# A padding of 32 bytes ahead of the arena in a two-block transformer kernel

## Chip, cores and metric

One core of a Trainium2 chip runs the kernel. The metric is device time in microseconds for one execution, lower is better.

## The reference

Two transformer blocks run on one sequence of 512 tokens with 1024 channels, in float32. The first block has two layers. Each modulates x by conditions, projects it (`h @ w_in`), and mixes three branches: attention over 512 latent and 256 context tokens, a depthwise convolution of 31 taps with a layer norm, and a pooling over windows of 2 to 16 tokens. Then comes a gated feed-forward part. Layer 0 treats the 256 context tokens as well, 768 tokens in all; layer 1 treats 512.

```python
def conv_ffn(h, w_up, dw_w, dw_b, w_down):
    a, u = jnp.split(h @ w_up, 2, axis=-1)
    a = depthwise_conv(a, dw_w, dw_b)
    return (jax.nn.silu(a) * u) @ w_down
```

The second block also has two layers: latent attention and gated linear attention side by side, an output product, and a gate of the residual: `h + sigmoid(rmsnorm(h) @ w_ple_gate) * (p @ w_ple_proj)`.

## The kernel before, in words

Activations lie with channels in the 128 partitions and tokens along the row: eight chunks of 128 channels, each `TOK` = 768 floats long. Every large product is done in three fp32r products, high part by high part, high by low and low by high. So an activation stands as a pair (`act_hi`, `act_lo`), and so does a weight (`w_hi`, `w_lo`). Weights come in units of 128 x 1024 floats (one output chunk): the SP queue loads a unit into `w_raw`, ACT rounds it to `w_hi` (line 1244), POOL or DVE subtracts to get `w_lo` (lines 479, 1931, 1937), and TensorE uses it. A ring of four units is in flight.

On TensorE a unit is eight chunks by three products. `unit` (line 595) issues them product by product; `first_pair` (line 530) interleaves the first two units of a stage that has to wait for its activations chunk by chunk; `first_four` (line 544) does it with four units and `unit_by_chunk` (line 644) with one. In layer 0 each chunk takes a matmul of 512 columns and one of 256 with the same weights; in layer 1 and in the second block one of 512.

```python
def unit(s, tile, sp_, kt, hi, lo, within=None):
    for n, (w, act) in enumerate(((WH, hi), (WL, hi), (WH, lo))):
        ...
        for k in range(kt):
            for a, b in sp_:
                last = nc.tensor.matmul(tile(a, b), w[:, s * UNIT + k * P:s * UNIT + (k + 1) * P],
                                        act[:, k * TOK + a:k * TOK + b],
```

The stages of a layer of the first block are, in order: conv, gate0, qkv, attn (and attn_ctx in layer 0), u, mix, gate2, gate1, pw, out, then up0, down0, up1, down1, up2, down2. The pool mixing (mix) multiplies fp32 operands of the arena (line 857). The feed-forward part has 22 chunks of 128, cut into parts of 8, 8 and 6. A stage up_p makes a part's chunks (16, 16 and 12 units), DVE convolves them (lines 2378, 2381), ACT applies silu (line 1574), DVE multiplies (line 2389) and splits the product into `ffn_hi` and `ffn_lo` (lines 1903, 1905), and the stage down_p multiplies these by eight units of 8, 8 and 6 chunks (line 877). DVE adds its result to x (line 1990). down_p begins with `first_pair`; its other six units come from `unit`. In down2 the sums of the layer norm stand between the units. The convolution's taps run on DVE beside the products (lines 2142, 2150): an even tap reads the arena at an offset of one float per tap.

In the second block the products are issued at line 902. Its last stage, pg, multiplies `u2_hi` and `u2_lo` by eight units in each of two layers.

Memory: tensors are laid one behind another in a partition, each start rounded up to 32 bytes. x, act_hi, act_lo, w_raw, w_hi, w_lo and tmp come first, and all start at multiples of 64. Some small tensors follow, then the masks, then the arena, 20280 floats, which is the last. It starts at 148192 = 64 x 2315 + 32. The names below are three views of the same memory:

```python
        ARENA_N = 20280
        with nc.sbuf_tensor("arena", [P, ARENA_N], f32) as AR:
            pass
        with nc.sbuf_tensor("ffn_hi", [P, CH * TOK], f32r) as GH, nc.sbuf_tensor("ffn_lo", [P, CH * TOK], f32r) as GL:
            pass
```

`u2_hi` and `u2_lo` follow in the same way. ffn_hi and u2_hi start where the arena starts; ffn_lo and u2_lo follow them by multiples of 64 bytes. Within the arena most operands lie at multiples of 16 floats. Exceptions are the convolution's sum and inputs, and the sums of the layer norms (offset 13832 = 16 x 864 + 8).

The order of the work is fixed by the program: each engine runs its own list, and semaphores hold it until its inputs are there.

Of the kernel before, what the change touches and what calls it, by code (L numbers as in the profile page):

```python
# [131 lines left out]
def two_blocks(nc, weights, ada_w, pool_w, vec1_d, vec2_d, gla_w_d, x_d, cond_d, ple_d, pos_d, consts_d, rope_d,  # L132
# [4 lines left out]
    with ctx:  # L137
        def sb(name, n, dt=f32):
            return ctx.enter_context(nc.sbuf_tensor(name, [P, n], dt))
# [28 lines left out]
        Q_EPS = CST[:, 3:4]  # L168
        MASK = sb("gla_masks", 2 * P, i32)
        ARENA_N = 20280  # L170
        with nc.sbuf_tensor("arena", [P, ARENA_N], f32) as AR:
            pass

# [35 lines left out]
        CLN_R = CONV_IN  # L209
        QR = ARENA_N - HEADS * TOK // P  # L210
        LN_R_BACK = CONV_SUM
# [2674 lines left out]
```

How the kernel before makes its waits and increments, by code:

```python
        @block.sync  # L399
# [7 lines left out]
            def unit_load(r, s):  # L407
                sp.wait_ge(units_split, r * SLOTS + s - 1)
                sp.dma_start(RAW[:, (s % 2) * UNIT:(s % 2 + 1) * UNIT],
                             weights[bass.ds(r * SLOTS + s, 1)].rearrange("o p n -> p (o n)")).then_inc(raw_landed[s % 2], 16)
# [8 lines left out]
            for i in range(ADA_FIRST // 2):
                ada_early_load(i)
            for dst, src in ((VEC1T, vec1_d), (IDENT, consts_d[0]), (PERM, consts_d[1]), (ONES, consts_d[2])):
                sp.dma_start(dst[:, :], src).then_inc(loaded, 16)
            sp.dma_start(RC[:, :], consts_d[3][:, 0:64]).then_inc(loaded, 16)
            for i in range(ADA_FIRST // 2, ADA_FIRST):
                ada_early_load(i)
            for s in range(2):
                sp.dma_start(RAW[:, s * UNIT:(s + 1) * UNIT], weights[s]).then_inc(raw_landed[s], 16)
            sp.wait_ge(on(0, "cond"), 1)
            for k, landed in enumerate((x_half, cond_loaded)):
                part = slice(k * CH // 2 * TOK, (k + 1) * CH // 2 * TOK)
                sp.dma_start(X[:, part], x_d[:, part]).then_inc(landed, 16)
# [16 lines left out]
                        unit_load(r + (RING[l, st] + (s + 3) // SLOTS), (s + 3) % SLOTS)  # L449
                        for a in range(first + s * n, first + (s + 1) * n):
                            sp.wait_ge(on(0, "ada_used"), r * (SLOTS * n // 2) + (a // 2 + ADA_STEPS - 1))
                            if a % ADA_SLOTS == 3:
```

## Time and profile before

| | us |
|---|---|
| median of 3 runs | 3226.6 |
| the runs | 3226.60, 3230.95, 3224.77 |
| span of the profiled execution, from the first to the last instruction | 3229.0 |
| TensorE busy in it | 3124.9 |
| DVE, ACT, POOL busy | 1947.2, 1140.8, 805.5 |

Of the profiled execution only the span is given; no time around it is shown. A matmul's record overlaps the next one's, since matmuls are pipelined, so the pace of a stage is read from starts and not from durations. In the timeline an entry merges neighbouring matmuls of the same operands, and x8 or x16 is a group: one product of a unit, eight chunks of 512 columns or eight pairs of 512 and 256.

### The profile page before, as it was taken

How to read it: one execution, taken by the hardware profiler on the slowest of the kernel's cores; microseconds unless marked ns; L12 is line 12 of the kernel's file. 1: busy time of each engine (PE TensorE's matmuls, PEld its weight loads, DVE VectorE, ACT ScalarE, POOL GpSimd, SP SyncE). 2: the span in 40 equal slices, each digit the busy share in tenths (PEclk: the TensorE clock that was granted, in tenths of full speed). 3: DMA queues.
4: the chain of work that ended last, by engine and by line, in shares of the span. 5: the costliest groups of instructions: out<-in, count | busy, mean ns of one | idle time of the engine just before them, and what ended most of it. 6: DMA issues, size and time to landing. Idle time of an engine off the chain costs nothing.

```text
span 3229.0 us, 43667 instructions
## 1 busy us (share of the span) xinstructions
PE 3124.9 (97%) x16074; PEld 2482.6 (77%) x16074; DVE 1947.2 (60%) x2707; ACT 1140.8 (35%) x1616; POOL 805.5 (25%) x316
## 2 busy tenths in 40 slices
PE   7999999999999999999999999999999999999998
PEld 4778877888878888886777677877886786777775
DVE  4787987654566154356978975663636565255443
ACT  3122254234232221124333535343223536343543
POOL 0001201232323232331012024402444322233312
PEclk9999999999999999999999999999999999999999
DMA  7442101112111211124531022422323221222211
GB/s 282 170 166 79 40 1 41 51 59 98 59 46 65 66 59 65 60 71 140 202 128 46 1 69 81 134 78 91 98 92 114 66 66 53 65 85 72 85 40 66
DMA packets 75308, 270.52 MB, mean 84 GB/s; under 512 B 8592, under 2 KB 9616, under 8 KB 74512
## 3 DMA queue, kind: packets, MB, share of 16 engines
q1 hardware_dynamic: 71376, 256.04, 23.9%
q10 hardware_dynamic: 3776, 12.32, 1.1%
q8 instruction: 108, 1.77, 0.2%
q14 instruction: 48, 0.39, 0.0%
HBM read 263.87 MB, written 4.46 MB: 83 GB/s over the span
## 4 chain that ended last, share of the span: by engine, by line
PE 86%; DVE 7%; ACT 2%; DVEq 2%; issue 1%; DMA 1%; SPq 0%; ACTq 0%
PE ps L595 50%; PE ps L902 11%; PE ps L530 4%; PE ps L544 2%; PE ps L711 2%; PE ps L834 2%; PE ps L1043 1%; PE ps L732 1%; PE ps L699 1%; PE ps L814 1%; PE ps L1122 1%; PE ps L644 1%; PE ps L602 1%; PE ps L1140 1%; PE ps L857 1%
## 5 line engine op out<-in xcount | busy, mean ns | idle before, releaser
L479 POOL TENSOR_TENSOR w_lo<-w_raw,w_hi 128x1024 fp32r<-128x1024 f32 x312 | 805.3, 2584 | 2389.3 <-ACT w_hi L1244 2389.3
L1244 ACT ACTIVATE w_hi<-w_raw 128x1024 fp32r<-128x1024 f32 x380 | 399.7, 1055 | 572.3 <-PE ps L595 304.8
L595 PE MATMUL ps<-act_hi,w_hi 128*128 128x512 f32 x2544 | 538.4, 361 | 2.3 <-DVE w_lo L1931 0.6
L595 PE MATMUL ps<-act_lo,w_hi 128*128 128x512 f32 x2544 | 521.8, 354 | 0.0
L595 PE MATMUL ps<-act_hi,w_lo 128*128 128x512 f32 x2544 | 521.2, 354 | 0.0
L595 PEld LDWEIGHTS ps<-act_hi,w_hi 128*128 128x128 f32 x2544 | 417.1, 188 | 117.3 <-issue 44.1
L595 PEld LDWEIGHTS ps<-act_hi,w_lo 128*128 128x128 f32 x2544 | 417.4, 188 | 70.3
L595 PEld LDWEIGHTS ps<-act_lo,w_hi 128*128 128x128 f32 x2544 | 417.2, 188 | 70.2 <-issue 0.5
L1990 DVE SCALAR_TENSOR_TENSOR x<-ps,mod,x 128x512 f32<-128x512 f32 x96 | 60.3, 659 | 295.3 <-PE ps L595 238.1
L2150 DVE SCALAR_TENSOR_TENSOR x<-arena,vec,x 128x512 f32<-128x512 f32 x336 | 230.5, 713 | 0.2 <-issue 0.2
L2142 DVE SCALAR_TENSOR_TENSOR arena<-arena,vec 128x783 f32<-128x783 f32 (+1 forms) x240 | 227.8, 949 | 0.0
L2381 DVE SCALAR_TENSOR_TENSOR arena<-arena,vec 128x769 f32<-128x769 f32 (+1 forms) x88 | 143.2, 1627 | 15.4 <-issue 15.4
L1310 ACT ACTIVATE arena<-ps,vec 128x768 f32<-128x768 f32 (+3 forms) x64 | 50.8, 794 | 278.6 <-PE ps L595 192.3
L902 PE MATMUL ps<-act_hi,w_hi 128*128 128x512 f32 x432 | 119.2, 408 | 7.3 <-ACT act_hi L1597 6.2
L2378 DVE TENSOR_SCALAR arena<-arena,vec 128x769 f32<-128x769 f32 (+1 forms) x44 | 29.1, 661 | 140.1 <-ACT arena L1569 140.1
L902 PE MATMUL ps<-act_hi,w_lo 128*128 128x512 f32 x432 | 113.1, 394 | 0.0
L902 PE MATMUL ps<-act_lo,w_hi 128*128 128x512 f32 x432 | 112.6, 392 | 0.0
L834 PE MATMUL ps<-arena 128*128 128x256 f32 (+1 forms) x288 | 103.7, 480 | 4.7 <-ACT tmp L1349 4.7
L1569 ACT ACTIVATE arena<-ps 128x512 f32<-128x512 f32 x66 | 32.4, 525 | 211.2 <-PE ps L595 201.0
L902 PEld LDWEIGHTS ps<-act_hi,w_hi 128*128 128x128 f32 x432 | 79.8, 190 | 34.5 <-issue 17.2
L1905 DVE TENSOR_TENSOR ffn_lo<-arena,ffn_hi 128x768 f32 (+1 forms) x44 | 101.3, 2302 | 6.5
L711 PE MATMUL ps<-arena 128*128 128x256 f32 x416 | 103.1, 381 | 1.6 <-ACT arena L1468 1.5
(343 smaller groups left out, 4490.5 us busy)
## 6 DMA issues: line engine op xcount, KB each, us to landing
w_raw<-in_weights SPq DMA_DIRECT2D x380, 512.0 KB, 3.5
arena<-in_ada_w SPq DMA_DIRECT2D x75, 512.0 KB, 4.7
tmp<-in_ada_w SPq DMA_DIRECT2D x21, 512.0 KB, 4.8
x<-in_x SPq DMA_DIRECT2D x2, 1536.0 KB, 20.0
x<-in_x ACTq DMA_DIRECT2D x1, 3072.0 KB, 10.4
arena<-in_pool_w ACTq DMA_DIRECT2D x2, 1024.0 KB, 4.9
x_mid<-x ACTq DMA_DIRECT2D x1, 2048.0 KB, 7.4
x<-x_mid ACTq DMA_DIRECT2D x1, 2048.0 KB, 8.5
```

The source lines that it names most:

```text
L479: nc.gpsimd.tensor_tensor(WL[:, w], raw, WH[:, w].bitcast(f32), ALU.subtract).then_inc(units_split, 1)
L530: last = nc.tensor.matmul(ps(tb + s, a, b), w[:, s * UNIT + k * P:s * UNIT + (k + 1) * P], act[:, k * TOK + a:k * TOK + b], start=(n == 0 ...
L544: last = nc.tensor.matmul(tile(0, s, a, b), w[:, s * UNIT + k * P:s * UNIT + (k + 1) * P], act[:, k * TOK + a:k * TOK + b], start=(n == 0 ...
L595: last = nc.tensor.matmul(tile(a, b), w[:, s * UNIT + k * P:s * UNIT + (k + 1) * P], act[:, k * TOK + a:k * TOK + b], start=(n == 0 and k ...
L711: last = nc.tensor.matmul(ps(3, (m % 2) * 512, (m % 2) * 512 + 2 * P), values(m, k), AR[:, a:a + 2 * P], start=(k == 0), stop=(k == nk - 1))
L834: last = nc.tensor.matmul(ps(it % 2, a, b), AR[:, q:q + P], AR[:, k + a:k + b], start=True, stop=True)
L902: return nc.tensor.matmul(out, w0[:, k0:k0 + P], act[:, k * n:k * n + SEQ], start=start, stop=stop)
L1244: nc.scalar.activation(WH[:, s * UNIT:(s + 1) * UNIT], RAW[:, (s % 2) * UNIT:(s % 2 + 1) * UNIT], ACT.Copy).then_inc(hi_done, 1)
L1905: return V.tensor_tensor(lo, src, hi.bitcast(f32), ALU.subtract)
L2142: t = V.scalar_tensor_tensor(acc, src, w, acc, ALU.mult, ALU.add)
L2150: t = V.scalar_tensor_tensor(acc, src, w, acc, ALU.mult, ALU.add)
L2381: t = V.scalar_tensor_tensor(cv, src, w, cv, ALU.mult, ALU.add)
```

## The change

A tensor of eight floats, 32 bytes in each partition, is laid between the masks and the arena. Nothing reads or writes it.

```diff
         Q_EPS = CST[:, 3:4]
         MASK = sb("gla_masks", 2 * P, i32)
         ARENA_N = 20280
+        sb("gap_before_arena", 8)
         with nc.sbuf_tensor("arena", [P, ARENA_N], f32) as AR:
             pass
```

The arena, ffn_hi and u2_hi then start at 148224 = 64 x 2316, which is also 256 x 579. All other tensors stay where they are.

## Rows read from the trace of the kernel before

**Rows 1.** The page: span; granted clock in 40 slices; chain by engine.

```profile
span 3229.0 us, 43667 instructions
...
PEclk9999999999999999999999999999999999999999
...
PE 86%; DVE 7%; ACT 2%; DVEq 2%; issue 1%; DMA 1%; SPq 0%; ACTq 0%
```

**Rows 2.** TensorE's waits: us in total, times, longest.

```profile
PE ps L732 <- DMA arena<-in_ada_w: 16.3, 3, 9.3
```

**Rows 3.** TensorE's groups by form: xcount | busy us, mean ns | idle.

```profile
L595 PE MATMUL ps<-ffn_hi,w_hi 128*128 128x512 f32 x264 | 82.1, 399 | 1.7 <-DVE x L1990 1.7
...
L902 PE MATMUL ps<-u_hi,w_hi 128*128 128x512 f32 x128 | 35.3, 399 | 2.3 <-ACT arena L1843 1.8 <-DVE arena L2723 0.5
...
L530 PE MATMUL ps<-ffn_hi,w_hi 128*128 128x512 f32 x88 | 30.9, 396 | 2.3 <-DVE arena L2389 2.3
```

**Rows 4.** TensorE's timeline, layer 1, down1 and up2: start us, us.

```profile
2356.85 2.03 PE L595 MATMUL ps<-ffn_hi,w_lo 128*128 128x512 f32 x8
...
2386.72 2.02 PE L595 MATMUL ps<-ffn_lo,w_hi 128*128 128x512 f32 x8
...
2392.24 1.98 PE L595 MATMUL ps<-act_lo,w_hi 128*128 128x512 f32 x8
...
2452.08 1.98 PE L595 MATMUL ps<-act_lo,w_hi 128*128 128x512 f32 x8
```

**Rows 5.** TensorE's timeline, second block, the gate product (pg).

```profile
2825.43 2.03 PE L902 MATMUL ps<-u_hi,w_lo 128*128 128x512 f32 x8
...
2844.10 2.03 PE L902 MATMUL ps<-u_lo,w_hi 128*128 128x512 f32 x8
```

**Rows 6.** TensorE's timeline, layer 0: down0, then up2.

```profile
1071.66 3.04 PE L595 MATMUL ps<-ffn_hi,w_hi 128*128 128x512 f32 x16 [0.36 <-DVE x L1990]
1074.54 2.96 PE L595 MATMUL ps<-ffn_hi,w_lo 128*128 128x512 f32 x16
...
1119.34 2.96 PE L595 MATMUL ps<-ffn_lo,w_hi 128*128 128x512 f32 x16
...
1400.73 2.94 PE L595 MATMUL ps<-act_hi,w_lo 128*128 128x512 f32 x16
...
1420.14 2.94 PE L595 MATMUL ps<-act_lo,w_hi 128*128 128x512 f32 x16
```

**Rows 7.** TensorE's timeline, layer 0: pw, out and up0.

```profile
779.68 3.05 PE L595 MATMUL ps<-act_hi,w_hi 128*128 128x512 f32 x16 [0.25 <-DVE arena L2315]
782.57 3.00 PE L595 MATMUL ps<-act_hi,w_lo 128*128 128x512 f32 x16
...
819.32 3.00 PE L595 MATMUL ps<-act_lo,w_hi 128*128 128x512 f32 x16
...
848.02 2.23 PE L595 MATMUL ps<-act_hi,w_hi 128*128 128x512 f32 x11 [0.27 <-DVE x L1990]
...
953.85 2.98 PE L595 MATMUL ps<-act_hi,w_lo 128*128 128x512 f32 x16
...
996.25 2.98 PE L595 MATMUL ps<-act_hi,w_lo 128*128 128x512 f32 x16
```

**Rows 8.** The chain in order of time: stage mix, layer 0.

```profile
599.79 20.64 PE ps L857 x64
```

**Rows 9.** Two lines of DVE: xcount: duration ns min/median/max.

```profile
L2142 DVE SCALAR_TENSOR_TENSOR arena<-arena,vec x69: 1023/1030/1036, 61.1 to 277.1; 128x783 f32<-128x783 f32 x69
...
L1905 DVE TENSOR_TENSOR ffn_lo<-arena,ffn_hi x44: 691/2655/3016, 953.1 to 2456.1; 128x768 f32 x22, 128x512 f32 x22
L1905 DVE TENSOR_TENSOR act_lo<-arena,act_hi x12: 691/692/694, 2546.4 to 3107.5; 128x512 fp32r<-128x512 f32 x12
```

**Rows 10.** The page, part 6: DMA issues, KB each, us to landing.

```profile
arena<-in_ada_w SPq DMA_DIRECT2D x75, 512.0 KB, 4.7
tmp<-in_ada_w SPq DMA_DIRECT2D x21, 512.0 KB, 4.8
```

## The prediction

> **What bounds the kernel.** I read the chain that ended last, then TensorE's waits, then its groups by form, then its timeline. The chain is TensorE for 86% of 3229.0 us [rows 1], and its waits are small: the largest is 16.3 us for the first loads [rows 2]. Its clock is granted in full, 2.4 GHz, in all 40 slices [rows 1]. So what counts is the spacing of matmuls in a full queue, and little else. The profiled execution's span, 3229.0 us, lies 2.4 us above the median of the runs, 3226.6; the sum below is a difference, set against the median. About 0.2% (6.5 us) is what a measurement can tell from no change; the three runs themselves lie 6.2 us apart.
>
> **What moves.** No instruction is added, dropped or moved. Every address in the arena, and so in ffn_hi, ffn_lo, u2_hi and u2_lo, grows by 32 bytes; all but a few arena operands go from 32 bytes past a multiple of 64 onto one. act_hi, act_lo, w_hi and w_lo lie on multiples of 64 before and after. The trace of before thus holds both cases of the same instruction.
>
> **Step 1: 512-column fp32r matmuls that stand alone (layer 1, second block).** Starts of groups of eight: from ffn_hi and ffn_lo 16 steps take 2386.72 - 2356.85 = 29.87 us, 1.867 each; from act_hi and act_lo 33 steps take 2452.08 - 2392.24 = 59.84 us, 1.813 each [rows 4]. The gate product from u2 gives 18.67 us in 10 steps, again 1.867 [rows 5]. So a misplaced moving operand costs 0.054 us in eight, 6.7 ns (three per cent) a matmul. Counts: ffn sources have (264 + 88) x 3 = 1056 matmuls of 512 columns over two layers, 528 of them in layer 1; u2 sources have 128 x 3 = 384 [rows 3]. That is 66 + 48 = 114 groups by 0.0535 = **6.1 us less**, all in stages where TensorE hardly waits (1.7, 2.3 and 2.3 us in the three groups [rows 3]). ACT, DVE and POOL deliver weights fast enough for 1.813, since the up stage between the down stages runs at it [rows 4].
>
> The Trainium skill ("TensorE: Matmul & The Clock Gate", section "Back-to-back issue gap") gives a warm matmul N / 2.4 + 2.5 ns, 215.7 ns for 512 columns, with no term for an address. By that rule this step would be worth nothing; the trace disagrees, with 226.7 and 233.3 ns for one shape.
>
> **Step 2: the pairs of layer 0 (512, then 256 columns).** Here the change may lose. Eight pairs from ffn take 44.80 / 16 = 2.800 us in down0; from act they take 19.41 / 7 = 2.773 in up2 [rows 6], but 36.75 / 13 = 2.827 in pw and 42.40 / 15 = 2.827 in up0 [rows 7]. Same instructions and placement, two rhythms, and each lasts for a stage or more. What differs is how the stage starts: pw and out (779.68, 848.02) begin after TensorE stood idle for 0.25 and 0.27 us behind the last first-pair matmul, and fall into the slow one [rows 7]. The down stages begin in just that way (1071.66, idle 0.36, behind x) [rows 6]. Once their operand is placed like act, I expect them at 2.827: 66 groups by 0.027 = **1.8 us more**. Stages up1 and up2 follow without a break. They have 16 + 12 units of three groups, 84, now at 2.773 (rows of up2 stand for both) [rows 6]; up0 held the slow rhythm through all of its units and loop turns [rows 7], so I expect it to be handed on: 84 x 0.0535 = **4.5 us more**.
>
> **Step 3: fp32 matmuls on the arena.** They take two cycles a column: 64 in stage mix, 32 pairs of 768 columns, take 20.64 us [rows 8], 0.645 a pair against 2 x 768 / 2.4 = 640 ns. An operand off its place shows no more than those 5 ns. I take nothing; the bound is 2.5 ns for each of roughly 1500 such matmuls (by the groups by form, those that run four at a time taken as one), 3.8 us less, and nothing excludes 0.5 more. The sums (arena offset 13832, the ln means) move the other way, off a multiple of 64; they are a few of these.
>
> **Step 4: DVE, ACT, POOL.** The taps of line 2142 read at 15 offsets 8 bytes apart and take 1023 to 1036 ns [rows 9], so DVE doesn't see placement. I take nothing; even 13 ns on each of some 1000 instructions lies beside matmuls.
>
> **Step 5: DMA.** 512 KB land in 4.7 us in the arena and 4.8 in tmp [rows 10]. TensorE waits for arena loads three times, 16.3 us, at the start [rows 2]. I take nothing, with 0.1 us for each wait, 0.3, either way.
>
> The Trainium skill ("DMA: Bandwidth & Descriptors", "How a descriptor splits into AXI transactions") says that a start off a 256-byte boundary costs extra beats. The arena goes from 224 past such a boundary onto one, so an estimate by that page is 135 beats falling to 128, 5% off its loads, under 1 us of the first loads' wait. No row here has a load onto such a boundary.
>
> **Sum.** -6.1 + 1.8 + 4.5 = +0.2 us: 3226.8.
>
> **Rivals.**
> (a) The down stages of layer 0 fall into the fast rhythm, so up1 and up2 keep it: -6.1 - 66 x 0.027 = -7.9, 3218.7. For it: up1 and up2 run so now, after ffn stages [rows 6]. Against: both act stages that begin after an idle run slow [rows 7]. 18%.
> (b) The slow rhythm takes the down stages alone, and breaks at the loops of up1 and up2, or in down1 where the start is perturbed: -6.1 + 1.8 = -4.3, 3222.3. 18%.
> (c) Slower: DVE against POOL. ffn_lo takes DVE 0.69 us or up to 3.02 for the same line, act_lo never over 0.69 [rows 9]; I read the long ones as DVE held up while POOL splits weights. A shifted rhythm changes which ones meet. The first pair of each down stage (line 530) waits for them, behind line 2389, now 2.3 us in all [rows 3]. One more on that path costs 3.02 - 0.69 = 2.3 us at most; it decides from three, for which there are six down stages: +0.2 + 6.9, 3233.7. Against: so many long ones exist now (the median is 2.66), and they cost 2.3 us. 6%.
> (d) Placement has no bearing, or the padding is swallowed so the arena stays where it is, and the 6.7 ns come from something else that ffn and u2 share: 3226.6. The Trainium skill's rule quoted in step 1 ends here as well. Against: two tensors, three stages, one figure. 6%.
> My own case has the remaining 52%.
>
> **How the numbers follow.** The time is that of my case. Low: (a) at 3218.7 less the first loads' 0.3 and rounding, 3218. High: my case with 0.5 + 0.3 of unknown costs and the spread of the runs (the highest 3230.95), 3230.5; it leaves out (c) and the lower part of (a). My case's own range is 3223 to 3230.5. Faster by over 0.2% means below 3220.1: nearly all of (a), a little of (b) and, by the bound of step 3, of mine: 0.23. Slower means above 3233.1: (c) and 1% for runs: 0.07. The same: 0.70.
>
> **What would show it.** Groups of eight from ffn in layer 1 and from u2 at 1.813 instead of 1.867 show step 1 right; at 1.867 they show (d). Groups of eight pairs in down0, down1 and down2 of layer 0 at 2.827 and in up1 and up2 at 2.827 show step 2 right; 2.773 in all shows (a), a mix shows (b). Line 857's 20.64 us, line 2142's 1030 ns and the 4.7 us of landing should stay. The forecast fails if the rhythm of layer 0 is set by more than the start, or if a stage that now runs at 2.773 from act (u, gate2) changes its rhythm too: some 48 groups, 2.6 us.

## The result, and the profile after

The change makes the kernel slower: 3233.7 us, median of 21 runs (3228.07 to 3237.16), against 3227.2 for the kernel before, also 21 runs in the same rounds (3223.65 to 3232.44). The ratio is 1.0020, 95% interval 1.0014 to 1.0026. The forecast was 3226.8 with a range of 3218.0 to 3230.5, and 0.07 on "slower". The profiled execution took 3234.3 us, 1.8 more than its span; its span is 3.5 us above that of before [rows 1]. In every run here the time is 1.8 us more than the span, so the profiled execution of before took about 3230.8 us, 3.6 above its median, and that of the change 0.6 above its own: the two profiles show about half of the difference of 6.5 us.

The page after: span, granted clock, chain by engine.

```profile
span 3232.5 us, 43667 instructions
...
PEclk9999999999999999999999999999999999999999
...
PE 86%; DVE 7%; ACT 2%; DVEq 2%; issue 1%; DMA 1%; SPq 0%; ACTq 0%
```

Clock, instruction count and the chain's shares are the same, and DVE and ACT are as busy as before (1947.2 and 1140.7 us), so what differs must lie mainly in how TensorE's matmuls are spaced. All lines past the edit are one higher. TensorE's groups by form (xcount | busy us, mean ns | idle), against [rows 3]:

```profile
L596 PE MATMUL ps<-ffn_hi,w_hi 128*128 128x512 f32 x264 | 81.9, 399 | 1.7 <-DVE x L1991 1.7
...
L903 PE MATMUL ps<-u_hi,w_hi 128*128 128x512 f32 x128 | 35.1, 399 | 2.3 <-ACT arena L1844 1.8 <-DVE arena L2724 0.5
```

Each is 0.2 us less; 6.7 ns on the 132 matmuls of the first that stand alone and on the 128 of the second would be 0.9 us. TensorE's timeline after (start us, us), layer 1 down1 and up2, then the gate product of the second block, against [rows 4, 5]:

```profile
2364.28 2.02 PE L596 MATMUL ps<-ffn_lo,w_hi 128*128 128x512 f32 x8
...
2392.16 2.02 PE L596 MATMUL ps<-ffn_lo,w_hi 128*128 128x512 f32 x8
...
2397.69 1.98 PE L596 MATMUL ps<-act_lo,w_hi 128*128 128x512 f32 x8
...
2424.89 1.98 PE L596 MATMUL ps<-act_lo,w_hi 128*128 128x512 f32 x8
...
2830.87 2.03 PE L903 MATMUL ps<-u_hi,w_lo 128*128 128x512 f32 x8
...
2849.53 2.04 PE L903 MATMUL ps<-u_lo,w_hi 128*128 128x512 f32 x8
```

Eight from ffn now take 27.88 / 15 = 1.859 us (1.867 before), eight from act 27.20 / 15 = 1.813, eight from u2 18.66 / 10 = 1.866. The operand stands on a multiple of 64 and has not become as fast as act. The timeline after for layer 0, up0, down0, the start of up1, and up2, against [rows 6, 7]:

```profile
955.10 2.93 PE L596 MATMUL ps<-act_hi,w_lo 128*128 128x512 f32 x16
...
1046.62 2.93 PE L596 MATMUL ps<-act_hi,w_lo 128*128 128x512 f32 x16
...
1073.97 2.97 PE L596 MATMUL ps<-ffn_hi,w_lo 128*128 128x512 f32 x16
...
1118.90 2.98 PE L596 MATMUL ps<-ffn_lo,w_hi 128*128 128x512 f32 x16
...
1124.53 2.99 PE L596 MATMUL ps<-act_hi,w_lo 128*128 128x512 f32 x16
...
1161.28 2.99 PE L596 MATMUL ps<-act_lo,w_hi 128*128 128x512 f32 x16
...
1328.13 2.99 PE L596 MATMUL ps<-act_hi,w_lo 128*128 128x512 f32 x16
...
1415.77 3.00 PE L596 MATMUL ps<-act_lo,w_hi 128*128 128x512 f32 x16
```

Eight pairs: up0 91.52 / 33 = 2.773 (2.827 before), down0 44.93 / 16 = 2.808 (2.800), up1 36.75 / 13 = 2.827 and up2 87.64 / 31 = 2.827 (2.773). So up1 and up2 lose 84 x 0.0535 = 4.5 us, as step 2 said, and step 1's 6.1 us to pay for it didn't come.

One more stage of layer 0 turned slow, gate1. Its last units that `unit` issues, before and then after, from a second group to the first matmul behind them:

```profile
732.12 2.94 PE L595 MATMUL ps<-act_hi,w_lo 128*128 128x512 f32 x16
754.31 0.51 PE L644 MATMUL ps<-act_hi,w_hi 128*128 128x512 f32 x2
...
732.85 2.98 PE L596 MATMUL ps<-act_hi,w_lo 128*128 128x512 f32 x16
755.46 0.51 PE L645 MATMUL ps<-act_hi,w_hi 128*128 128x512 f32 x2
```

Eight groups take 22.19 / 8 = 2.774 before and 22.61 / 8 = 2.826 after; with the unit that follows and pw's first pair it costs 0.9 us.

### The profile page after: what moved, and what is told of

Same layout as the page of the kernel before. It is cut to its first block, busy times and chain, and to the rows that moved or that the text cites. A ratio compares the mean times of both kernels' runs of the same rounds, so it can differ in the third digit from the quotient of the medians.

```text
span 3232.5 us, 43667 instructions
## 1 busy us (share of the span) xinstructions
PE 3130.7 (97%) x16074; PEld 2484.4 (77%) x16074; DVE 1947.2 (60%) x2707; ACT 1140.7 (35%) x1616; POOL 803.8 (25%) x316
## 4 chain that ended last, share of the span: by engine, by line
PE 86%; DVE 7%; ACT 2%; DVEq 2%; issue 1%; DMA 1%; SPq 0%; ACTq 0%
PE ps L596 50%; PE ps L903 11%; PE ps L531 4%; PE ps L545 2%; PE ps L712 2%; PE ps L835 2%; PE ps L1044 1%; PE ps L700 1%; PE ps L733 1%; PE ps L815 1%; PE ps L1123 1%; PE ps L645 1%; PE ps L603 1%; PE ps L1141 1%; PE ps L858 1%
```

## The experiments

Two questions: what separates 226.7 from 233.3 ns, if not the multiple of 64, and whether the slow rhythm of up1 and up2 is the whole loss. "Distance" below is the moving operand's address less the weights', modulo 256 bytes. act_hi and act_lo lie at 41088 and 65664, w_hi at 98432, w_lo at 114816, all with remainder 128; ffn_hi and u2_hi at 148192 before (distance 96) and 148224 after (distance 128).

### m1_addresses: the same matmul at 18 addresses

A kernel of its own: one tensor over all of SBUF, matmuls of 512 columns of fp32r on it, `w(address, k)` the weights and `m(address, k)` the moving operand of chunk k, nothing beside TensorE.

```python
59: for r, k, e in steps(12): last = mm(o(r), w(98432, k), m(148192, k), **e)
60: ...                                  w(98432, k), m(148224, k)
61: ...                                  w(98432, k), m(41088, k)
62: ...                                  w(98432, k), m(41120, k)
63: ...                                  w(98432, k), m(41152, k)
67: ...                                  w(98432, k), m(148352, k)
```

> Not the kernel: 28 stretches of 512-column fp32r matmuls with nothing else running on the core, each stretch on its own line, eight chunks per group, weights at 98432 unless the line says otherwise. Theory H (height): what sets the time is whether the moving operand lies above 128 KiB: about 226.7 ns a matmul for the lines at 41088 to 127104, about 233 ns for those from 131200 up, whatever the remainder. Theory M (remainder): what sets it is the address modulo 256 beside that of the weights: 226.7 ns for 41088, 65664, 90240 and 148352 (remainder 128 as the weights'), 233 for the others, low ones too. Theory O (other): the 6.7 ns come from what runs beside or around the matmuls of ffn and u2: all lines at 226.7 ns. The misplacement theory of the prediction, that 32 bytes off a multiple of 64 cost 6.7 ns: 41120, 41184 and 148192 at 233, all others at 226.7.

The timeline; a line's 96 matmuls end where the next line starts:

```profile
95.98 22.58 PE L59 MATMUL ps<-sbuf 128*128 128x512 f32 x96
118.39 22.48 PE L60 MATMUL ps<-sbuf 128*128 128x512 f32 x96
140.71 21.95 PE L61 MATMUL ps<-sbuf 128*128 128x512 f32 x96
162.49 22.57 PE L62 MATMUL ps<-sbuf 128*128 128x512 f32 x96
184.90 22.15 PE L63 MATMUL ps<-sbuf 128*128 128x512 f32 x96
206.88 22.57 PE L64 MATMUL ps<-sbuf 128*128 128x512 f32 x96
...
274.08 21.94 PE L67 MATMUL ps<-sbuf 128*128 128x512 f32 x96
295.87 22.15 PE L68 MATMUL ps<-sbuf 128*128 128x512 f32 x96
```

The address that ffn has in the kernel before (L59): (118.39 - 95.98) / 96 = 233.4 ns. The one that it has after the change (L60): 232.5. act's (L61): 226.9. With nothing else running the kernel's own three figures are there (1.867, 1.859 and 1.813 us per eight are 233.4, 232.4 and 226.7 ns), so ffn's slowness isn't contention. Theory H, height, is out: 148352, above 128 KiB, runs at 227.0 (L67), 41120, below, at 233.4 (L62). A multiple of 64 isn't it either: 148224 is one. Theory M stands for all with remainder 128, but 41152 (remainder 192) took 229.0 (L63), which it had at 233. The weights had remainder 128 in all lines, so M and a rule of distance are not yet told apart. Nor is distance all of it to the nanosecond: 41216 has distance 128, as 148224 has, and took 233.3 where that took 232.5.

### e1_gap_front: everything 32 bytes up

```diff
+        sb("gap_before_x", 8)
         X = sb("x", CH * TOK)
```

with no gap ahead of the arena, which so lies where the change puts it.

> The 32 bytes stand ahead of x instead of ahead of the arena: the arena lies where it does after the change, but x, act, the weights, tmp and all tables move by 32 bytes too, and act and the weights are now 32 bytes off a multiple of 64. If the arena's address alone made the change's +6 us: 3233 us. If operands off a multiple of 64 cost 6.7 ns a matmul: act is read by some 8000 of them, so +50 us, 3280. If only the distance between arena and weights counts: as before, 3227.

3226.1 us (11 runs), ratio 0.9996 (0.9987 to 1.0005). act and the weights are now 32 bytes off a multiple of 64, and the arena is on one, and the time is that of before. In its profile ffn's eight take 1.867 us and up1 and up2 run at 2.773, as before. So neither the arena's own address nor being off a multiple of 64 costs the 6 us; the distance, 96 again, fits.

### e2_arena_160: distance 0

```diff
-        ARENA_N = 20280
+        ARENA_N = 20240
+        sb("gap_before_arena", 40)
```

> A gap of 160 bytes instead of 32, so that the arena has the remainder 128 modulo 256 that act and the weights have. Theory M (remainder): ffn and u2 matmuls at 226.7 ns, 1.813 us per eight, 6.1 us back: near 3221 to 3227. Theory H (height above 128 KiB) or O: 232 to 233 ns, and 3227 to 3234 according to the rhythm that layer 0 falls into.

The timeline: layer 1 down1; layer 0 down0; layer 0 up2.

```profile
2355.54 1.98 PE L596 MATMUL ps<-ffn_lo,w_hi 128*128 128x512 f32 x8
...
2382.74 1.98 PE L596 MATMUL ps<-ffn_lo,w_hi 128*128 128x512 f32 x8
...
1073.47 2.94 PE L596 MATMUL ps<-ffn_hi,w_lo 128*128 128x512 f32 x16
...
1117.84 2.94 PE L596 MATMUL ps<-ffn_lo,w_hi 128*128 128x512 f32 x16
...
1324.60 3.00 PE L596 MATMUL ps<-act_hi,w_lo 128*128 128x512 f32 x16
...
1420.71 3.00 PE L596 MATMUL ps<-act_lo,w_hi 128*128 128x512 f32 x16
```

Eight from ffn: 27.20 / 15 = 1.813, what step 1 had forecast for the change. The gate product has it too: 16.32 us in 9 steps (2822.09 to 2838.41), 1.813. Pairs run at 44.37 / 16 = 2.773 in down0 and at 2.773 in up1; but down1 begins in the slower rhythm (45.23 / 16 = 2.827, from 1273.72) and up2 follows at 96.11 / 34 = 2.827. The time is 3224.8 (3220.15 to 3229.01, 11 runs), ratio 0.9993 (0.9984 to 1.0002).

### e3_after_again: the change once more

> The change as it is, once more. If its rhythm in up1 and up2 of layer 0 (2.827 us per eight pairs, 2.773 before) belongs to the layout, it is there again and the time is 3233 to 3234. If the rhythm is a matter of chance in each run, up1 and up2 can be at 2.773 here.

3235.2 us (9 runs), ratio 1.0024 (1.0014 to 1.0034). The profiled run was the longest of them, 3238.6. up1 and up2 at 2.827 again; but up0 at 2.827 (2.773 in the first profile) and stage u at 2.773 (2.827). So u and up0 differ from run to run with one layout, while up1 and up2 (and gate1, 2.826) came out as in the first profile.

### m2_distances: weights moved too, and smaller steps

```python
59: ... w(98464, k), m(41120, k)      60: ... w(98464, k), m(41088, k)
61: ... w(98496, k), m(41088, k)      62: ... w(98560, k), m(41088, k)
63: ... w(98560, k), m(41216, k)      71: ... w(98432, k), m(41156, k)
```

> Not the kernel: 512-column fp32r matmuls (and 512+256 pairs) by themselves, one line per pair of addresses. Theory D (distance): the spacing hangs on the moving operand's address minus the weights', modulo 256, and on neither address alone. So: both moved by 32 (41120 with 98464) 226.7 ns; weights at 98464 with 41088 (distance 224) 233.3; weights at 98496 (192) 233.3; 98560 (128) 232 to 233; 41216 with 98560 (distance 0) 226.7; distances of 256, 512, 1024 and 2048: 226.7. Theory M (the moving operand's own remainder): 41088 at 226.7 with all weights, 41120 at 233. On the rhythm of pairs, theory R (handed on): pairs at distance 0 that follow pairs at distance 128 run at 2.827 us per eight, those that follow pairs at distance 96 or 0 at 2.773. Rival: pairs at distance 0 run at 2.773 here whatever stood before them, and the kernel's slower rhythm comes from the other engines.

```profile
97.25 21.95 PE L59 MATMUL ps<-sbuf 128*128 128x512 f32 x96
119.04 22.57 PE L60 MATMUL ps<-sbuf 128*128 128x512 f32 x96
141.44 22.56 PE L61 MATMUL ps<-sbuf 128*128 128x512 f32 x96
163.84 22.47 PE L62 MATMUL ps<-sbuf 128*128 128x512 f32 x96
186.15 21.98 PE L63 MATMUL ps<-sbuf 128*128 128x512 f32 x96
207.97 22.89 PE L64 MATMUL ps<-sbuf 128*128 128x512 f32 x96
...
364.62 23.20 PE L71 MATMUL ps<-sbuf 128*128 128x512 f32 x96
387.65 22.36 PE L72 MATMUL ps<-sbuf 128*128 128x512 f32 x96
```

Both up by 32 (L59): (119.04 - 97.25) / 96 = 227.0 ns; weights alone up by 32 (L60): 233.3; both up by 128 (L63): 227.3; weights alone (L62): 232.4. Theory M falls, D holds. By their start-to-start times, distances of 0, 256, 512, 1024 and 2048 bytes gave 226.7 ns; 32, 96, 192 and 224 gave 233.3; 64 gave 228.9; 128 gave 232.3 to 233.4; 160 gave 234.2. Steps off a multiple of 32 run from 226.7 (240 and 252 bytes) to 240.0 (68 bytes, L71: 239.9).

The same run's pairs at distance 0, from the timeline per eight: behind pairs at distance 128, 2.827, each of four times; behind pairs at distance 96, 2.773; behind 64, 2.773; behind 192, 2.827. The rhythm is handed on with no other engine at work.

### e4_ffn_old_place: the change, but ffn back

```diff
-        sb("gap_before_arena", 8)
-        with nc.sbuf_tensor("arena", ...) as AR:
+        with nc.sbuf_tensor("gap_before_arena", [P, 8], f32), nc.sbuf_tensor("arena", ...) as AR:
             pass
...
-        LN_SQ = (6 * TOK, 7 * TOK, (CH + 6) * TOK, (CH + 7) * TOK)
+        LN_SQ = tuple(a - 8 for a in (6 * TOK, 7 * TOK, (CH + 6) * TOK, (CH + 7) * TOK))
```

The gap ends with the arena's own block, so ffn_hi starts at 148192 again; u2 gets a gap of its own and stays at 148224.

> The change, with the copies ffn_hi and ffn_lo alone (and the four squares that lie in them) back at their address of before (148192), all else in the arena 32 bytes higher, u2 among it. Theory R: the downs of layer 0 run at 2.800 us per eight pairs as before, up1 and up2 at 2.773 as before, so 4.5 us of the change's 6 are gone: 3227 to 3229. Rival (the slower rhythm of up1 and up2 comes from the rest of the arena, its vectors and sums, or from chance): 3233, with up1 and up2 at 2.827.

```profile
1071.08 2.96 PE L595 MATMUL ps<-ffn_hi,w_lo 128*128 128x512 f32 x16
...
1115.88 2.96 PE L595 MATMUL ps<-ffn_lo,w_hi 128*128 128x512 f32 x16
...
1121.46 2.94 PE L595 MATMUL ps<-act_hi,w_lo 128*128 128x512 f32 x16
...
1154.74 2.94 PE L595 MATMUL ps<-act_hi,w_lo 128*128 128x512 f32 x16
```

down0 at 44.80 / 16 = 2.800, up1 at 33.28 / 12 = 2.773, up2 the same. 3226.4 us (11 runs), ratio 0.9995 (0.9986 to 1.0004). With all the rest of the arena moved the loss is gone, to within the 0.1% that these runs tell, so most of it came through ffn's distance. Not all: gate1 runs at (754.45 - 731.84) / 8 = 2.826 here too, with ffn back. It did so in all five profiles with the arena 32 bytes up and the weights in place (the change, e3, e4, e5, e7), and at 2.773 or 2.774 in the other five (before, e1, e2, e6, e8). Between gate1's units stand fp32 matmuls that read the arena (lines 602 and 610); whether they hand it the rhythm was not tested.

### m3_resets and m4_from_fast: what turns the rhythm

Slow pairs at distance 0, one small thing, then 40 pairs at distance 0. Two of the cases, a pair with its 256 columns first (lines 63 and 64) and one extra matmul of 256 columns (87); the pairs behind them are at lines 66 and 89.

```python
63: for r, k, e in steps(1)[:1]:
64:     for a, b in ((512, 768), (0, 512)): last = mm(o(r, a, b), w(98432, k), m(41088, k, a, b), ...)
...
87: for r, k, e in steps(1)[:1]: last = mm(o(r, 0, 256), w(98432, k), m(41088, k, 0, 256), ...)
```

> Not the kernel: 512+256 pairs at distance 0, each time first brought into the slow rhythm (2.827 us per eight) by pairs at distance 128 (148224), then one small disturbance, then pairs again. Theory R: the rhythm is a phase that the matmuls keep and hand on, so a disturbance in their order can throw it back to 2.773; in the run before, eight 256-column or eight 384-column matmuls did, one or two 512-column ones did not. Which of the smaller ones do (a single pair with its 256 first, one to four matmuls of 128, 256 or 384 columns) is open: those that do are followed by 2.773, the others by 2.827. Rival: the rhythm follows from what was moved long before and no small thing changes it: all at 2.827. Pairs in alternating order (512, 256, 256, 512) have no forecast.

```profile
117.39 14.29 PE L66 MATMUL ps<-sbuf 128*128 128x512 f32 x80
131.51 11.40 PE L68 MATMUL ps<-sbuf 128*128 128x512 f32 x64
...
222.52 14.03 PE L89 MATMUL ps<-sbuf 128*128 128x512 f32 x80
236.40 11.39 PE L91 MATMUL ps<-sbuf 128*128 128x512 f32 x64
```

Per eight pairs: (131.51 - 117.39) / 5 = 2.824 behind the turned pair, (236.40 - 222.52) / 5 = 2.776 behind the one extra matmul. One extra matmul of 128, 256 or 384 columns led to 2.773; so did two or four of 128, and four of 384; two, three or four of 256, two of 384 and one to three of 512 did not. A phase that the stream keeps and one extra matmul can shift would do this; the records show the spacing alone, so the phase is an inference. Pairs with the 256 columns first throughout ran at 2.787 at distances 0 and 128 and at 2.800 at 96.

> Not the kernel: pairs at distance 0, now brought into the fast rhythm (by pairs at distance 96) as well as into the slow one (by pairs at distance 128), then one matmul of 32 to 512 columns, then pairs again. From the slow rhythm a 128-column matmul is expected to lead to 2.773 us per eight again; 16 to 64 columns have no forecast. From the fast rhythm theory R leaves it open whether a nudge of 128 columns stays fast (then it can be put ahead of any stage) or throws it into 2.827 (then it helps only where the rhythm is known to be slow).

From the fast rhythm one of 128 columns led into the slow one; one of 256, 384 or 512 stayed fast; one of 32 or 64 led to 2.773 from either, and one of 16 from the slow one. Straight behind pairs at distance 128 a 128-column one led into the slow rhythm, and so did one that came one or four pairs later; two or three pairs later it led into the fast one.

### e5_change_nudged, e6_160_nudged: a nudge in the wrong place

```diff
+                if nudge:
+                    start(0, 0)
+                    nc.tensor.matmul(tile(0, 0, 0, P), WH[:, 0:P], hi[:, 0:P], start=True, stop=True)
                 if ready:
```

> The change, with one more matmul of 128 columns ahead of the first group of up1 and of up2 in layer 0; its product is overwritten by the group's own start. Nothing moves in SBUF. Theory R (the downs at distance 128 hand the slow rhythm on): up1 and up2 go from 2.827 to 2.773 us per eight pairs, 84 groups by 0.053 is 4.5 us back, less some 0.1 us for each matmul: 3229 to 3230, beside 3234 to 3235 for the change. Rival (the arena's address slows up1 and up2 themselves, by the vectors or copies that run beside them): up1 and up2 stay at 2.827, time 3234.

```profile
1129.85 3.00 PE L599 MATMUL ps<-act_hi,w_lo 128*128 128x512 f32 x16
1132.68 3.00 PE L599 MATMUL ps<-act_lo,w_hi 128*128 128x512 f32 x16
...
1333.52 2.94 PE L599 MATMUL ps<-act_hi,w_lo 128*128 128x512 f32 x16
1336.30 2.94 PE L599 MATMUL ps<-act_lo,w_hi 128*128 128x512 f32 x16
```

The extra matmuls stand at 1126.92 and 1330.63. up1 stayed slow (2.83 us from group to group), up2 became fast (2.78); both hold to the end of the stage. 3233.4 us (12 runs), ratio 1.0016 (1.0007 to 1.0024); the profiled run was the longest, 3239.2. One stage of two: a miss in the time, and in line with m4, run beside it, that the spot straight behind the downs is a poor one.

> The gap of 160 bytes (distance 0), with one more matmul of 128 columns ahead of up2 of layer 0, whose profiled run had 353.3 ns a pair there. Theory R: 346.7 ns a pair in up2, 1.9 us less than 3224.8, so 3223. If the nudge meets the fast rhythm in some runs and throws it into the slow one: no gain over 3224.8.

up2 at 2.773 in the profiled run (3219.9 us), but the median is 3226.2 (3219.72 to 3234.64), ratio 0.9997 (0.9987 to 1.0006): no gain over the gap alone. The second case of what was expected fits the spread; a single profile can't show it.

### e7_change_nudged_in: most of the loss undone without moving anything

```diff
+                elif nudged:
+                    for s in range(SLOTS):
+                        if s == 1:
+                            nudge(0, 1)
+                        single(0, s)
+                    with loop(pe, rounds - 1) as j:
...
```

> The change, with one extra matmul of 64 columns between the first and the second unit of up1 and of up2 in layer 0, so behind 24 pairs at distance 0 and not straight behind the downs, as the run by itself found that a nudge right behind pairs at distance 128 can land in the slow rhythm again, and one of 16 to 64 columns after some pairs at distance 0 led to the fast one from either. Nothing moves in SBUF. Theory R: 24 pairs at 353.3 ns, then 346.7 ns to the end of each stage; (384 + 288 - 48) x 6.7 ns = 4.2 us back, less 2 x 0.09: about 3230, if the change alone takes 3234. Rival: 353.3 ns throughout, 3234.

```profile
1127.99 0.19 PE L570 MATMUL ps<-act_hi,w_hi 128*128 128x64 f32 x1
...
1130.88 2.94 PE L615 MATMUL ps<-act_hi,w_lo 128*128 128x512 f32 x16
...
1161.39 2.94 PE L615 MATMUL ps<-act_hi,w_hi 128*128 128x512 f32 x16
```

Behind the nudge 30.51 / 11 = 2.774; its own cost is the 0.09 us by which the group after it is longer. 3228.0 us (11 runs), ratio 1.0003 (0.9994 to 1.0012), against 1.0020 (1.0014 to 1.0026) for the change. By these ratios, each taken beside its own runs of before, two matmuls of 64 columns take back 5.5 us of 6.5, give or take some 3; 4.2 was expected. The rhythm of up1 and up2 is most of the loss; gate1 still runs at 2.826 here.

### e8_160_nudged_in: all of it together

The gap of 160 bytes, and e7's nudge in u, gate2, gate1, pw, out and all up and down stages of layer 0.

> The gap of 160 bytes (distance 0 for ffn and u2), with the same 64-column matmul after the first units of u, gate2, gate1, pw, out, up0 to up2 and down0 to down2 in layer 0, 11 of them. Theory: all pairs of these stages at 346.7 ns but the first units, ffn and u2 singles at 226.7 ns. Against before: 6.1 us from ffn and u2 singles, 1.7 us from 510 pairs of the downs (350.0 to 346.7), 4.3 us from the 650 or so pairs of pw, out and up0 that ran at 353.3 in part, less 11 x 0.09: about 11 us, 3217. Rival: a nudge throws as many stages into the slow rhythm as it brings out of it: 3222 to 3225, as the gap of 160 bytes alone.

The profiled run took 3219.0 us, span 3217.2, with u, gate2, down0, up1, down1 and up2 at 2.773 throughout, and so the last units of gate1, pw and up0; out ran at 2.827 for eight groups, and down2 slow in part. The median is 3225.5 (11 runs), ratio 0.9993 (0.9984 to 1.0002). That is just above the rival's 3222 to 3225 and far from 3217. So no version here is shown to beat the kernel before; e2, e6 and e8 beat the change. In e2, e6 and e8 the median lies 3 to 6.5 us above the profiled run; where the other runs lose that stayed open.

## Why the prediction was wrong, point by point

**Step 1 failed, and the sign of the sum with it.** It took "off a multiple of 64" for what parts act from ffn and u2, and booked -6.1 us. ffn went from 1.867 to 1.859, 0.4 us in all, and the gate product stayed. Act and ffn differed in several ways: height, remainder modulo 64, modulo 256, distance to the weights. The trace of before held two cases, which can't choose among them. m1, m2 and e1 showed the last: distance 0 modulo 256 gives 226.7 ns, distance 96 gives 233.3, and 128 gives 232.3 or 233.3. Which of these two appears at 128 stayed open; ffn got the lower, the gate product, at the same start, the upper. The change goes from one slow distance to another; e2, at distance 0, has the 1.813. Rival (d) said this in part ("something else that ffn and u2 share"), but had nothing move in layer 0, and so no loss; it got 6%. The forecast of "about the same" came from setting a gain that didn't exist against a loss that did.

**Step 2 held in its main term and in the handing on, not in where the rhythm came from.** up1 and up2 were forecast at 2.827 and are, in three profiles (the change, e3, and e5's up1), for the forecast 4.5 us; that they take it over from the down stages is shown by m2 and e4, and that it is most of the loss, by e7. The reason given for the downs was wrong. They don't run at 2.827 like act but at their own 2.808 at distance 128, so that term is 66 x 0.008 = 0.5 us and not 1.8. Nor does a start behind a short idle make a stage slow: out begins after the same 0.27 us and runs at 2.827 before [rows 7] but at 2.773 in the profile after (852.49 to 874.68, eight groups), and pw at 2.773 in e1. And where the operand truly lay like act, in e2, down0 and up1 ran at 2.773, down1 and up2 at 2.827. What turned up1 and up2 slow was pairs at distance 128 ahead of them, behind which pairs at distance 0 ran at 2.827 each time. So the 4.5 us were right in part by luck.

**Steps 3 to 5 held in what they measured.** Stage mix takes 20.64 us as in [rows 8], the taps of line 2142 1022 / 1029 / 1035 ns against [rows 9], ffn_lo a median of 2.66 as in [rows 9], and loads into the arena land in 4.6 us (4.7 before [rows 10]; those into tmp, which didn't move, went from 4.8 to 5.1, so 0.1 tells nothing). Two things they left out. The fp32 matmuls on the arena keep their own pace, but gate1, whose units alternate with some of them, turned slow (0.9 us). And the first loads are not good to 0.3 us: the first matmuls of stage conv start 0.7 us earlier than before in the profile of the change and 2.7 us later in e3's, with one layout. Rival (c) named the right time (3233.7) by luck: ffn_lo takes what it took, and the first pairs of the down stages moved by nothing like 6.9 us.

**The range.** Its top doesn't follow from what it names: 3226.8 + 0.8 and a highest run 4.4 us above the median make 3232.0, not 3230.5. The 2.4 us between the span and the median set two different measures side by side; with the 1.8 us above, that run was 3.6 us over the median.

**The sum as it came.** The two profiles of the change can be laid over that of before matmul by matmul, by their starts. What both show in much the same size: up1 +2.5 and up2 +1.9, together the 4.5; gate1 +0.9; the stages from qkv to attention +0.3 and +0.5; down0 and down1 +0.3; the singles from ffn -0.4. That is about 5.6 us, where the medians say 6.5. Two more, +0.7 in and behind down2 and +0.9 in one spot of layer 1 (near 1690), are in both but not in e5's profile, so whether they belong to the layout stayed open. The rest is run to run: in the first profile up0 is 1.9 us shorter than before and stage u 1.2 longer, and in e3 both are as before. That, the first loads and the second block (1.6 us shorter) bring the first profile to 3.5 us. The last paragraph of the prediction named a risk of this kind (an act stage that changes rhythm) at 2.6 us, for u and gate2; the stage that changed with the layout was gate1.

The Trainium skill ("TensorE: Matmul & The Clock Gate", section "Back-to-back issue gap") gives N / 2.4 + 2.5 ns for a matmul by itself, about 216 ns for 512 columns, and about 131 ns a matmul for a stream of them. No fp32r matmul of 512 columns in these runs was that near its successor at a steady rate: 226.7 was the least, and the distance of the two addresses decided between that and 240.0.

## What to carry to other kernels

When one shape runs at two speeds in a trace, list everything in which the two cases differ, and move each by itself in a small kernel with only that engine, before a price is put on one of them; here the property that counts was a relation between two operands (moving and weights the same modulo 256 bytes), not a place of one. A loop of unequal matmuls can have two steady rhythms: where a stage is bound by TensorE, read the spacing per stage on both sides, and expect an edit in one stage to reach the next through it. A difference of 0.2% is not seen in one profile of each kernel: single stages (u, up0) and the first loads differed by 1.2 to 3.4 us between two runs of one kernel here; the medians of 21 runs told the change from the kernel before, and 9 to 12 runs were good to 0.1%.

## What the runs showed of the hardware

- fp32r matmuls of 512 columns at the full clock start 226.7 ns apart where the moving operand and the weights have the same address modulo 256, 228.9 at a distance of 64, 232.3 to 233.4 at 32, 96, 128, 192 and 224, 234.2 at 160, up to 240.0 at 68. Moving both by the same amount changed nothing (m1, m2).
- Matmuls of 384 columns: 173.4 ns at distance 0, 176.7 at 96. Of 256 columns the other way: 120.0 at 0 and at 96, 118.6 at 128 (m2).
- Pairs of 512 and 256 columns at distance 0 have two steady rhythms, 2.773 and 2.827 us per eight, and pass them on over a change of stage, tile and loop turn (m2, e2, e3); one extra matmul of 64 columns between pairs led to the faster one from both (m4), for 0.09 us (e7).
